# Down units between every gate and up unit, also over the ends of passes, and one down row in four left plain: a mixture-of-experts kernel on one core

## The reference

```python
def hier_moe(x, norm_w, wg, bg, we, be, w_gate, w_up, w_down):
    h = rms_norm(x, norm_w).reshape(-1, D)            # 256 tokens, D = 2048
    ...                                               # top-1 of 4 groups, then top-2 of its 4 experts
    y = jnp.zeros((T, D), jnp.float32)
    for e in range(N_EXPERTS):                        # 16 experts, inner width 512
        a = jax.nn.silu(h @ w_gate[e]) * (h @ w_up[e])
        y = y + combine[:, e:e + 1] * (a @ w_down[e]).astype(jnp.float32)
    return x + y.reshape(B, S, D).astype(x.dtype)
```

## Time and profile before

| | |
|---|---|
| median of 3 executions | 1600.03 us |
| the profiled execution | 1598.73 us, of which its span is 1596.9 us |
| TensorE busy with matmuls | 95% of the span |
| VectorE, ScalarE busy | 79%, 62% |
| mean granted TensorE clock | 0.987 of full speed |
| bytes read from memory | 468.30 MB, 296 GB/s over the span |

### The profile page before, as it was taken

The page is one execution under the profiler, slowest core; times in us unless marked ns, Lnnn a source line. Parts: engine busy times, 40 slices in busy tenths (PEclk is TensorE's granted clock), DMA queues, the critical chain, the costliest instruction groups (busy, mean ns, idle before and its releaser), DMA issues.

```text
span 1596.9 us, 20533 instructions
## 1 busy us (share of the span) xinstructions
PE 1517.5 (95%) x6622; PEld 1091.2 (68%) x6622; DVE 1255.6 (79%) x1677; ACT 983.4 (62%) x1294; POOL 12.1 (1%) x23
## 2 busy tenths in 40 slices
PE   8999899998999999999999999899999999999998
PEld 8997894676666666666666667666666666666665
DVE  4898989756879688697978856788878869787884
ACT  5444342354768577576757754576767756776772
POOL 0000100000000000000000000000000000000000
PEclk9999999999999999999999999999999999999999
DMA  8973542443899899999989983289989999998993
GB/s 235 368 238 126 175 142 81 157 166 128 323 335 394 320 356 388 365 335 371 397 320 362 400 329 106 80 322 347 395 321 352 396 361 337 370 393 322 364 400 135
DMA packets 159755, 471.53 MB, mean 295 GB/s; under 512 B 20922, under 2 KB 40844, under 8 KB 159284
## 3 DMA queue, kind: packets, MB, share of 16 engines
q1 hardware_dynamic: 158148, 466.85, 79.1%
q10 hardware_dynamic: 1520, 3.59, 0.6%
HBM read 468.30 MB, written 4.21 MB: 296 GB/s over the span
## 4 chain that ended last, share of the span: by engine, by line
PE 70%; DVE 17%; issue 7%; ACT 5%; DMA 1%; SPq 0%; DVEq 0%; ACTq 0%
PE ps L2332 14%; DVE split_lo L1187 11%; PE ps L2299 10%; PE ps L1941 8%; PE ps L1943 8%; PE ps L1942 8%; PE ps L2300 7%; PE ps L2316 4%; PE ps L2022 3%; ACT split_hi L743 2%; PE ps L2248 1%; PE ps L2352 1%; ACT cat L743 1%; PE ps L1887 1%; PE ps L1922 1%
## 5 line engine op out<-in xcount | busy, mean ns | idle before, releaser
L1187 DVE TENSOR_TENSOR split_lo<-ring,split_hi 128x1024 fp32r<-128x1024 f32 x732 | 856.4, 1212 | 195.0 <-ACT split_hi L743 189.6
L743 ACT ACTIVATE split_hi<-ring 128x1024 fp32r<-128x1024 f32 x732 | 747.3, 1053 | 331.0 <-PE ps L1943 254.7
L2299 PE MATMUL ps<-split_hi,cat 128*128 128x512 f32 x1024 | 437.9, 428 | 50.8 <-DVE split_lo L1187 50.5
L2300 PE MATMUL ps<-split_lo,cat 128*128 128x512 f32 x1024 | 407.6, 398 | 0.0
L2299 PEld LDWEIGHTS ps<-split_hi,cat 128*128 128x128 f32 x1024 | 194.4, 190 | 190.6 <-DVE split_lo L1187 144.4
L2332 PE MATMUL ps<-ring,work 128*128 128x512 f32 x512 | 230.1, 592 | 0.0
L2300 PEld LDWEIGHTS ps<-split_lo,cat 128*128 128x128 f32 x1024 | 195.7, 191 | 30.1
L1941 PE MATMUL ps<-split_hi,cat 128*128 128x512 f32 (+1 forms) x464 | 205.7, 443 | 3.9 <-DVE cat L1187 3.8
L1943 PE MATMUL ps<-split_hi,cat 128*128 128x512 f32 (+1 forms) x464 | 179.9, 388 | 0.0
L1942 PE MATMUL ps<-split_lo,cat 128*128 128x512 f32 (+1 forms) x464 | 179.4, 387 | 0.0
L2332 PEld LDWEIGHTS ps<-ring,work 128*128 128x128 f32 x512 | 96.9, 189 | 97.4 <-issue 91.9
(11 more groups left out here) (237 smaller groups left out, 1186.3 us busy)
## 6 DMA issues: line engine op xcount, KB each, us to landing
ring<-in_w_gate SPq DMA_DIRECT2D x128, 1024.0 KB, 6.6
ring<-in_w_up SPq DMA_DIRECT2D x128, 1024.0 KB, 7.1
ring<-in_w_down SPq DMA_DIRECT2D x128, 1024.0 KB, 7.0
ring<-in_w_in_e SPq DMA_DIRECT2D x16, 1024.0 KB, 7.5
ring<-in_w_out_e SPq DMA_DIRECT2D x16, 1024.0 KB, 5.2
ring<-in_w_in_e SPq DMA_DIRECT2D x30, 512.0 KB, 5.1
ring<-in_pool_w_o SPq DMA_DIRECT2D x4, 1024.0 KB, 10.1
ring<-in_w_in_e SPq DMA_DIRECT2D x12, 256.0 KB, 6.1
```

The costliest lines, as they stand in the source:

```text
L743: return nc.scalar.activation(out, in_, ACT.Copy, scale=scale)
L1187: return tt(dst, full, hi.bitcast(F32), ALU.subtract)
L2299: mm(ps[:, bank, :], tokens, hi[:, k, :], start=q == 0 and k == 0, stop=False)
L2300: last = mm(ps[:, bank, :], tokens, lo[:, k, :], start=False, stop=q == 7 and k == 1)
```

## The change

`UNITS` becomes three lists. The first pass begins with g0 alone; every pass then runs u0, g1, d0, u1, g2, d1, u2, g3, d2, u3, g0 of the next pass, d3; the last pass, which has no next, ends u3, d2, d3. In a down unit the plain block's first half is now split too: 6 split halves and 4 plain matmuls, 36 fp32r matmuls, in the order k0, k1, plain, k2 for each pair of blocks. `actT` holds three turned rows instead of two, `actT32` one instead of two.

```diff
-UNITS = [(0, "g"), (0, "u"), (1, "g"), (0, "d"), (1, "u"), (2, "g"), (1, "d"), (2, "u"), (3, "g"), (3, "u"),
-         (2, "d"), (3, "d")]
+FIRST = [(0, "g")]
+EARLY = [(0, "u"), (1, "g"), (0, "d"), (1, "u"), (2, "g"), (1, "d"), (2, "u"), (3, "g")]
+MID = EARLY + [(2, "d"), (3, "u"), (EPG, "g"), (3, "d")]
+LAST = EARLY + [(3, "u"), (2, "d"), (3, "d")]
...
-        actT = [cat_cut(2 * D + i * HALF, 2, P) for i in range(2)]
+        actT = [cat_cut(2 * D + i * HALF, 3, P) for i in range(2)]
...
+                    def down(e, order, between=lambda n: None):
+
+                        pe.wait_ge(m["actT_out"], p * EPG + (e + 1))
                         for half in range(2):
+                            if e == 0 and not first_pass:
+                                pe.wait_ge(m["x_moved"], p * 4 + (2 * half - 1))
+                            banks = [ps[:, BANK_Y + 2 * half + n, :] for n in range(2)]
+                            for k in (0, 1, 3, 2):
+                                if k == 3:
+                                    j = 4 * order.index((e, "d")) + 2 * half + 1
+                                    wait_landed(pe, l, p, j)
+                                    w = raw_half(moe_slot(l, j), 1).rearrange("p (n c) -> p n c", n=2)
+                                    for n in range(2):
+                                        mm(banks[n], actT32[:, e % 2, :], w[:, n, :], start=False, stop=False)
+                                    continue
+                                between(3 * half + k)
+                                w = weights(2, 512)
                                 for n in range(2):
+                                    last = product(banks[n], pick_parts(actT[e % 2], ALL, k), pick_parts(w, ALL, n),
+                                                   e == 0 and k == 0, e == EPG - 1 and k == 2)
                                 last.then_inc(m["used"], 1)
...
+                    def beside_down3(n):
+
+                        if n == 1:
+                            choose_slots(p + 1)
+                        if n == 2:
+                            fold(p, EPG, "g")
```

More of the change, by code:

```diff
@@ L65, with split_units, units_before, unit_table @@
 EXTRA = 4
-UNITS = [(0, "g"), (0, "u"), (1, "g"), (0, "d"), (1, "u"), (2, "g"), (1, "d"), (2, "u"), (3, "g"), (3, "u"),
-         (2, "d"), (3, "d")]
+FIRST = [(0, "g")]
+EARLY = [(0, "u"), (1, "g"), (0, "d"), (1, "u"), (2, "g"), (1, "d"), (2, "u"), (3, "g")]
+MID = EARLY + [(2, "d"), (3, "u"), (EPG, "g"), (3, "d")]
+LAST = EARLY + [(3, "u"), (2, "d"), (3, "d")]
 BANK_U, BANK_T, BANK_Y = 2, 3, 4
-BANK_M = 1
+BANK_M, BANK_P = 1, 0
 SCATTER = ((0, 0), (1, 0), (0, 1), (1, 1))
 NPASS = (1 + EXTRA) * NG
[L75 to L93, removed]
+HEAD_BLOCKS = 4
+HEAD_UNITS = 8
+def split_units(order, j):
+    return 1 if order[j // 4][1] == "d" and j % 2 else 2
+def units_before(order, j):
+    return sum(split_units(order, i) for i in range(j))
+PASS_UNITS = units_before(MID, PASS_BLOCKS)
+def unit_table(order):
+    return [(j, h) for j in range(4 * len(order)) for h in range(split_units(order, j))]
 def fold_number(e, kind):
@@ new lines, in one_pass @@
+                    gate(p, 2)
+                    split(p, 45, 46)
+                    slots_lo(p, 3)
+                    split(p, 46, 57)
+                    times_up(2, 57)
+                    if last_pass:
+                        split(p, 57, 62, LAST)
+                        turned_lo(2)
+                        split(p, 62, 66, LAST)
+                        gate(p, 3)
+                        split(p, 66, 72, LAST)
+                        times_up(3, 72)
+                        split(p, 72, 76, LAST)
+                        turned_lo(3)
+                        split(p, 76, 80, LAST)
+                        y_lo(p, 0)
+                        return
@@ L1820, in one_pass @@
+                    split(p, 57, 62)
+                    turned_lo(2)
+                    split(p, 62, 67)
+                    gate(p, 3)
+                    split(p, 67, 68)
+                    if first_pass:
+                        dve.wait_ge(m["route_done"], 1)
+                    slots_lo(p + 1, 0)
+                    split(p, 68, 79)
+                    times_up(3, 79)
+                    split(p, 79, 84)
                     turned_lo(3)
-                    split(p, 78, 80)
-                    if last_pass:
-                        y_lo(p, 0)
+                    split(p, 84, 86)
@@ L2287, in project @@
                         bank = e % 2 if kind == "g" else BANK_U
-                        if kind == "g" and not (first_pass and e == 0):
+                        first = first_pass and (e, kind) == (0, "g")
+                        if kind == "g" and not first:
                             pe.wait_ge(m["gather_out"], p * EPG + (8 + e))
@@ L2292, in project @@
                             hi, lo = weights(2, 512)
-                            if first_pass and (e, kind) == (0, "g"):
+                            if first:
                                 pe.wait_ge(m["gather_out"], q + 1)
@@ new lines, in beside_up0, with beside_gate1 @@
+                            if q == 5:
+                                pe.wait_ge(sorted_out, 8 * l + 4)
+                                choose_slots(0)
+                        elif q == 5:
+                            scatter(p - 1, 0)
+                    def beside_gate1(q):
+                        if not first_pass:
+                            if q == 0:
+                                scatter(p - 1, 1)
+                            if q == 1:
+                                scatter(p - 1, 2)
+                            if q == 4:
+                                scatter(p - 1, 3)
+                        if q == 3:
+                            fold(p, 0, "u")
+                        if q == 6:
+                            turn_act(0)
+                            turn_pick()
```

480 lines of the change are left out of this document (242 added, 238 removed).

## The result

| | before | after |
|---|---|---|
| median, eight executions each | 1600.03 us | 1606.51 us (1605.04 to 1611.58) |
| ratio to before | | 1.0043 (95% interval 1.0029 to 1.0058) |
| the profiled execution, its span | 1598.73, 1596.9 us | 1608.32, 1606.4 us |
| mean granted TensorE clock | 0.987 | 0.976 |

A forecast was written before the change was run, and what follows sets the result against it. TensorE and VectorE wait for each other, VectorE's splits pacing gate and up units, so time sums intervals between down units. Savings of 9.6 us per layer, 19.2 in all, took 1598.7 to 1579.5, so 1580 us; range 1555 to 1605.

The forecast's parts named there:

- the multiplication: VectorE's multiplication step between resuming its splits and the next down unit, counted at 0.66 us.
- the four middle passes: Passes neither first nor last in a layer: each forecast at 137.7 us for 139.40, 1.7 us less.
- the two first ones: Each layer's first pass: forecast to gain 4.5 us, mostly from `later_rounds` moving into d1.
- the last ones: Each layer's last pass: forecast to gain 2.2 us, over d0 to d1, the long interval, d2 and d3.
- the first d0: First down unit of a layer: forecast about 0.5 us later, for the low part and turns ahead of it.
- from there to the next down unit: VectorE's 15 splits (17.06 us), multiplication and low part after resuming: next down unit starts 31.5 us after the last.
- the low part: VectorE's making of the turned rows' low part before a down unit, now 384 columns, counted at 0.52 us.
- resuming at 13.20 us: VectorE starts the split of u.3 13.17 us into a down unit, once d.5 is used at 11.88 us.
- 33.8 for 33.2 and 42.2 for 41.5: Intervals d0 to d1, forecast 33.2 us, and d3 to the next d0, over a pass end, forecast 41.5.
- The rival of the late low part: Down units wait for the low part behind VectorE's splits, 1.14 us later in 30 of 32: 1614 us, chance 0.15.
- `later_rounds` lies hidden in d1: First pass: its 2.84 us of VectorE fall where VectorE stands still, saving 3.74 us less 0.9.
- Transfers: DMAs of a pass: 125.8 us at 400 GB/s, hidden; the skill's 358 GB/s would give 140.6, 1603 us total.

The follow-up runs named there:

- E10: Changed kernel with the down unit of before (two plain rows), its gate fold and tanh placed as before, and g.5 split ahead of the multiplication: 1588.07 us, 0.9929 of before.
- E1: Changed kernel with the multiplication back behind VectorE's split of g.5 in all experts but the last of a layer's last pass: 1595.09 us, 0.9970 of before.
- E11: Kernel before with one move, the multiplication ahead of VectorE's split of g.5 for experts 0 to 2: 1629.61 us, 1.0188 of before.
- E4: Changed kernel with three unneeded 128x512 matmuls ahead of g.5, where TensorE waits, in every gate unit but a layer's first: 1594.48 us, 0.9971 of before.
- E9: Changed kernel with three unneeded 128x512 matmuls ahead of g.1, where TensorE doesn't wait, leaving the wait ahead of g.5: 1603.52 us, 1.0020 of before.
- E3: Changed kernel with g.5 split ahead of the multiplication and the low part of the turned rows made ahead of the split of d.1: 1564.27 us, 0.9793 of before.
- E8: Changed kernel with fold, multiplication, turn_act and low part earlier for experts 1 to 3; for expert 0, g.5's split and low part earlier: 1560.36 us, 0.9737 of before.

## Why the prediction was wrong

Three kernels take the change apart: the order alone (E10) gives -11 to -12 us; the one plain row in four on top of it (E1) takes 7 back; the multiplication ahead of g.5 (the changed kernel) takes 11.4 more. Against the forecast, the profiled execution is 28.8 us too long (1608.3 to 1579.5): 15.0 in the four middle passes, 4.5 in the two first ones, 1.9 in the last ones, 7.4 ahead of the first d0.

**The step that failed** is "from there to the next down unit". It summed VectorE's work up to the start of the down unit, 31.5 us, and took TensorE's own way to end "at about the same time" without summing it and without asking when g.5 comes. So the multiplication's move ahead of g.5 was free in the sum. But TensorE gets g.5 later by 0.87 us, and behind g.5 come `turn_act`, g.6 and g.7; it stands 0.8 us right ahead of `turn_act`. Where TensorE's way is the path, that lengthens each interval by 0.86 us (E11). In the changed kernel it doesn't, since VectorE's way up to the low part ends as late (E1 has 31.9 us without the move); there it costs through the clock.

**The clock** is the largest part, and no term or rival had it. The wait of 0.8 us ahead of `turn_act` brings the half-clock stretches: E4 fills it and they go, E9 doesn't and they stay, E1 and E11 take it out and put it in. Five in the middle passes are 7.0 of the 15.0 us there, all nine some 11.7 of the 28.8. The sizes below make 11.1 in the passes, and 6.0 stand ahead of the first d0.

**The sizes.** Without stretches a pass is 139.8 us (E4), 2.1 more than counted. An inner interval is 31.83 for 31.48: resuming at 13.20 us (13.17 counted), the multiplication 0.87 (0.66 counted, although nearly hold it: the 12 splits end at 772.12, so the last starts at 770.91, and the next split follows at 772.90, 1.99 us later in place of 1.14, which makes 0.85), the low part 0.55 (0.52), 0.17 to the first matmul (0.07). The same misses stand in each interval; 33.8 for 33.2 and 42.2 for 41.5 have 0.3 to 0.4 more of their own, which no run takes apart. The gain is a difference of large sums, and 0.35 to 0.75 us in an interval took 11.1 of the 19.2 us forecast.

**The rival of the late low part** came true in part. In the changed kernel TensorE stands openly for the low part only over pass ends (0.86 us), since within a pass the late g.5 hides it. E1, where g.5 comes early, shows it: 0.64 us of TensorE's wait at a start and 1.7 over a pass end. E3, which removes both, is 31 us faster than E1. So the one plain row, with its shorter down unit, does pay, but only where the low part comes early: E3 is 24 us below E10, E1 7 us above it.

**What held.** VectorE's resume at 13.2 us. `later_rounds` lies hidden in d1, more fully than forecast: that interval is 31.75 us, with the stall gone. That E10 reaches a pass of 137.91 us, where 137.7 was forecast for the whole change, is luck: it has two plain rows, and its 33.58, 31.70, 31.68 and 40.95 us miss the forecast's 33.2, 31.5, 31.5 and 41.5 on both sides.

**Transfers.** By the table in the Trainium skill, "DMA: Bandwidth & Descriptors", "Specifications", the prediction estimated a time of 1603 us, with 358 GB/s for a core. The runs disagree: E8 moves 367 GB/s over a whole pass (361) and takes 1560 us, so that figure doesn't bound this kernel, which runs on one core.

**Left open.** Of the 7.4 us ahead of the first d0 one stretch in g1 makes about 1.4. 5.3 stand already at the first matmul of g0 (396.39 us for 391.06), behind a mixer that the change doesn't touch; the clock's record has some 24 us at half clock there, 14 before. Why the clock differs there isn't shown; the first d0 started at 427.8 to 438.0 us in the kernels here. Why nine of the 30 `turn_act` with the wait ahead of them bring a stretch and the others don't isn't shown either. Whether the small matmuls are needed for it was not tried apart.

## What to carry to other kernels

Where two engines feed each other, sum both ways to the point where they meet, in the order of each queue: a step that costs its own engine nothing can delay what the other has queued behind it. When two ways end together, moving either alone leaves the interval as it is; move both before calling a change worthless. And price a wait on TensorE by what stands next to it: the one of 0.8 us ahead of `turn_act` cost the changed kernel nothing in its intervals by itself and some 12 us through the clock.

## What the runs showed of the hardware

The clock fell behind a wait of 0.8 us followed by eight small matmuls (64x128, 2.1 us), though the record of the 2.4 us ahead of the fall shows TensorE busy throughout (the windows above). Three matmuls of 128x512 in the wait, 0.68 us of work, kept it at 2.4 GHz from a layer's first `turn_act` on (E4). Waits of 0.64 and 1.7 us at the start of down units brought no fall (E1). The Trainium skill, "TensorE: Matmul & The Clock Gate", section "A second HAM failure mode: psum-queue depth-cycling", tells of a kernel in which frequent short idles between groups of matmuls make the clock oscillate. These runs agree in part: short idles are enough here too, though the idle of 0.8 us comes once in an interval of some 32 us, and only nine of 30 of them brought a fall.
